# Gate and up projections of two FFNs: seven block products in place of eight

## The reference, cut to what matters

```python
D_MODEL, SEQ, D_FF = 1024, 512, 2816

def swiglu(x, w_gu, w_down):
    gu = x @ w_gu
    g, u = jnp.split(gu, 2, axis=-1)
    return (jax.nn.silu(g) * u) @ w_down

x = x + 0.5 * swiglu(rms_norm(x, g_ffn1), w_ffn1_gu, w_ffn1_down)
...
x = x + 0.5 * swiglu(rms_norm(x, g_ffn2), w_ffn2_gu, w_ffn2_down)
```

## Time and profile before

| what | us |
|---|---|
| time, median of 3 runs (1751.65 to 1751.79) | 1751.66 |
| profiled execution, its own time | 1754.53 |
| its span, first to last instruction | 1752.7 |
| PE busy in the span (9322 matmuls) | 1742.0 |
| DVE busy | 1039.4 |
| ACT busy | 760.7 |
| POOL busy | 431.9 |

### The profile page before, as it was taken

One profiled execution on the slowest core, in us unless ns is written; L12 is line 12 of the kernel. 1 busy time (PEld: TensorE's weight loads), 2 busy tenths in 40 slices (PEclk: granted clock), 3 DMA queues, 4 the chain that ended last, 5 costly groups with the idle time before them and its releaser, 6 DMA issues.

```text
span 1752.7 us, 25465 instructions
## 1 busy us (share of the span) xinstructions
PE 1742.0 (99%) x9322; PEld 1437.8 (82%) x9322; DVE 1039.4 (59%) x2178; ACT 760.7 (43%) x1413; POOL 431.9 (25%) x336
## 2 busy tenths in 40 slices
PE   9999999999999999999999999999999999999998
PEld 7778878777888888888888888889888888888887
DVE  5888867688867665555433455446756655555332
ACT  6566645556654533333232454555444322333222
POOL 4566644465553500000000332320200200000000
PEclk9999999999999999999999999999999999999999
DMA  6422123332212433333333422223321333333332
GB/s 198 138 88 73 60 61 98 95 95 79 73 49 62 138 109 96 96 96 96 106 101 106 151 64 93 85 84 103 103 64 58 96 96 96 96 96 96 109 107 85
DMA packets 54998, 166.20 MB, mean 95 GB/s; under 512 B 10264, under 2 KB 10776, under 8 KB 54904
## 3 DMA queue, kind: packets, MB, share of 16 engines
q1 hardware_dynamic: 53896, 163.69, 30.8%
q10 hardware_dynamic: 1008, 1.28, 0.2%
HBM read 162.25 MB, written 2.17 MB: 94 GB/s over the span
## 4 chain that ended last, share of the span: by engine, by line
PE 99%; DMA 0%; DVE 0%; ACT 0%; POOL 0%; SPq 0%; issue 0%; POOLq 0%
PE proj L1182 80%; PE turned L1514 2%; PE o L1536 2%; PE proj L1678 1%; PE proj L1671 1%; PE o L1779 1%; PE o L1879 1%; PE turned L1148 1%; PE turned L1758 1%; PE score L1483 1%; PE score L1868 1%; PE turned L1741 1%; PE score L1472 1%; PE score L1348 0%; PE proj L1382 0%; PE score L1741 0%
## 5 line engine op out<-in xcount | busy, mean ns | idle before, releaser
L1182 PE MATMUL proj<-hhi,whi 128*128 128x512 f32 x1456 | 580.8, 399 | 0.0
L1182 PE MATMUL proj<-hhi,wlo 128*128 128x512 f32 x1456 | 568.4, 390 | 0.0
L1182 PE MATMUL proj<-hlo,whi 128*128 128x512 f32 x1456 | 567.4, 390 | 0.0
L1970 ACT ACTIVATE whi<-ring 128x1024 fp32r<-128x1024 f32 x278 | 294.2, 1058 | 613.6 <-PE proj L1182 593.8
L2495 DVE TENSOR_TENSOR wlo<-ring,whi 128x1024 fp32r<-128x1024 f32 x199 | 243.0, 1221 | 161.7 <-ACT whi L1970 161.2
L1182 PEld LDWEIGHTS proj<-hhi,whi 128*128 128x128 f32 x1456 | 274.0, 188 | 61.3 <-issue 7.3
L1182 PEld LDWEIGHTS proj<-hhi,wlo 128*128 128x128 f32 x1456 | 273.4, 188 | 58.8
L1182 PEld LDWEIGHTS proj<-hlo,whi 128*128 128x128 f32 x1456 | 274.1, 188 | 53.0
L884 POOL TENSOR_TENSOR wlo<-ring,whi 128x512 fp32r<-128x512 f32 x160 | 213.9, 1358 | 331.7 <-ACT whi L1970 331.4
L902 POOL TENSOR_TENSOR prob<-prob 128x512 f32<-128x512 f32 x36 | 56.8, 1579 | 871.2 <-ACT prob L1966 871.2
L1996 ACT ACTIVATE prob<-prob,negmax 128x128 f32<-128x128 f32 (+3 forms) x208 | 114.0, 550 | 80.5 <-DVE negmax L2568 80.1
(11 more groups left out here) (402 smaller groups left out, 2470.1 us busy)
## 6 DMA issues: line engine op xcount, KB each, us to landing
ring<-wstream SPq DMA_DIRECT2D x285, 512.0 KB, 3.6
arena<-lines SPq DMA_DIRECT2D x28, 256.0 KB, 5.4
out<-arena SPq DMA_DIRECT2D x8, 256.0 KB, 3.3
...
```

What stands on the lines that cost most here:

```text
L1182: mm = pe.matmul(b, rounded(w), rounded(rhs(v, k)), start=(first and n == 0 and p == 0), stop=(last and n == len(blocks) - 1 and p == 2))
L1970: act.activation(rounded(dst), src, ACT.Copy, scale=scale).then_inc(ready, 1)
```

## The change

Of the 22 pairs of gate and up chunks, the first two (`PEEL`) stay as they were. For the other 20 (`SEVEN`) a pair is taken as a 2x2 block product: rows are gate and up, the contraction is split into two sets of four 128-feature blocks, and the tokens into two halves of 256. Seven products of four blocks are made in place of eight: `A11`, `S1`, `S2`, `A12`, `S3`, `S4`, `A22`, each 12 matmuls of 128x256 (four blocks, three parts). Their right sides are blocks of the activations or the combinations `T_1` to `T_4`, made once per FFN from a float32 copy `hx` of the activations (ACT `scale_h`, DVE `combine_h`, 128x1024 each; low parts of two of them on GpSimd). Their left sides are blocks of the weights or the sums `S1` to `S4`, made per pair by GpSimd (128x512 each, `seven_sums`). Each left side is rounded by ACT (`high_w`) and its low part made: `A11`, `S1`, `A12`, `A22` on VectorE (`low_w`), `S2`, `S3`, `S4` on GpSimd. PSUM sums are added up across products in place, with copies of the states in between by ACT (128x256, `copy`) and three additions by VectorE. There is one buffer for each of these operands, so the next pair's `S1` waits for PE's product `S1` of this pair (`sop_done`), and so on. A load into a pair's two ring slots now waits for the low part of `A22`. The nine early loads of `bias2` move from before the first FFN to the end of its gate and up part, and `norm_first` moves behind that part.

The diff, cut to its core (blank lines dropped):

```diff
+PEEL = 2
+SEVEN = FC - PEEL
+W_A11, W_S1, W_S2, W_A12, W_S3, W_S4, W_A22 = range(7)
+T_1, T_2, T_3, T_4 = range(4)
+HALF_S = S // 2
...
+            def load_ffn(n0, j0, f):
+                for s in range(4):
+                    sp.wait_ge(job_done, j0 + s + 1)
+                    load(stream_of(n0) + s + RING, s)
+                with sp.Fori(1, FC // 2) as i:
                     for s in range(4):
-                        sp.wait_ge(job_done, i * 4 + (j0 + s + 1))
+                        if s % 2 == 0:
+                            sp.wait_ge(slo_ready, i * 8 + (SLO + 4 * (f * SEVEN + s // 2 - 2) + 4))
                         load(i * 4 + (stream_of(n0) + s + RING), s)
+                if f == 0:
+                    sp.wait_ge(job_done, j0 + 2 * FC)
+                    sp.wait_ge(inner_done, FC)
+                    load_bias2(range(B2_EARLY))
                 load2(n0 + 2 * FC, n0 + FFN_SLOTS)
...
+            def seven_sums(i, s, n0, j0, f):
+                ahead = isinstance(i, int) and i == 0
+                g = f * SEVEN + s - 1
+                gate, up = 2 * (1 - s), 2 * (1 - s) + 1
+                pool.wait_ge(wload[up], i * 16 + 16 * (n0 // RING + 1 + s))
+                if not ahead:
+                    pool.wait_ge(sop_done, i * 12 + (SOP + 6 * (g - 1) + W_S1 + 1))
+                pool.tensor_tensor(ssum[W_S1], weight_quarter(up, 1), weight_quarter(up, 2), ALU.add).then_inc(sum_made, 1)
+                pool.wait_ge(wload[gate], i * 16 + 16 * (n0 // RING + 1 + s))
+                pool.wait_ge(sum_made, i * 8 + (SUM + 4 * g + 1))
+                if not ahead:
+                    pool.wait_ge(sop_done, i * 12 + (SOP + 6 * (g - 1) + W_S2 + 1))
+                pool.tensor_tensor(ssum[W_S2], ssum[W_S1], weight_quarter(gate, 1), ALU.add).then_inc(sum_made, 1)
+                if ahead:
+                    low_t(f, T_2)
+                else:
+                    pool.wait_ge(sop_done, i * 12 + (SOP + 6 * (g - 1) + W_S3 + 1))
+                pool.tensor_tensor(ssum[W_S3], weight_quarter(gate, 1), weight_quarter(up, 1), ALU.add).then_inc(sum_made, 1)
+                pool.wait_ge(sum_made, i * 8 + (SUM + 4 * g + 2))
+                if ahead:
+                    pool.wait_ge(job_done, j0 + 2 * PEEL)
+                else:
+                    pool.wait_ge(sop_done, i * 12 + (SOP + 6 * (g - 1) + W_S4 + 1))
+                pool.tensor_tensor(ssum[W_S4], ssum[W_S2], weight_quarter(gate, 2), ALU.add).then_inc(sum_made, 1)
+                pool.wait_ge(sum_made, i * 8 + (SUM + 4 * g + 4))
+                for w in (W_S2, W_S3, W_S4):
+                    pool.wait_ge(shi_ready, i * 14 + (SHI + 7 * g + w + 1))
+                    pool.tensor_tensor(slo[w].bitcast(F32R), ssum[w], shi[w], ALU.subtract).then_inc(pool_slo_ready, 1)
+            def low_t(f, t):
+                pool.wait_ge(thi_ready, THI + 4 * f + t + 1)
+                pool.wait_ge(t_ready, TC + 4 * f + 4)
+                pool.tensor_tensor(rounded(tlo[:, t, :]), tsum[:, t, :], thi[:, t, :], ALU.subtract).then_inc(pool_tlo_ready, 1)
+            def ffn_sums(n0, j0, f):
+                low_t(f, T_1)
+                seven_sums(0, 1, n0, j0, f)
+                with pool.Fori(1, FC // 2 - 1) as i:
+                    for s in range(2):
+                        seven_sums(i, s, n0, j0, f)
+                seven_sums(FC // 2 - 1, 0, n0, j0, f)
...
+                def seven(i, s):
+                    b = (j0 + s) % 2
+                    X, Y, Z = proj[b][:, 0:HALF_S], score[s][:, 0:HALF_S], opsum[s][:, 0:HALF_S]
+                    g = f * SEVEN + s - 2
+                    def product(to, w, parts, first):
+                        for k in range(KC // 2):
+                            for p, (weight, v) in enumerate(((shi[w], parts[0]), (shi[w], parts[1]), (slo[w], parts[0]))):
+                                mm = pe.matmul(to, rounded(weight[:, k, :]), rounded(v[:, k, :]), start=(first and k == 0 and p == 0),
+                                               stop=(k == KC // 2 - 1 and p == 2), skip_group_check=True)
+                        return mm
+                    h11, h21, h22 = ((quarter(hhi, j, l), quarter(hlo, j, l)) for j, l in ((1, 1), (2, 1), (2, 2)))
+                    t1, t2, t3, t4 = ((by_pair(thi, t), by_pair(tlo, t)) for t in range(4))
+                    pe.wait_ge(job_free[b], i * 2 + (j0 + s) // 2)
+                    pe.wait_ge(slo_ready, i * 8 + (SLO + 4 * g + 1))
+                    product(X, W_A11, h11, True).then_inc(sop_done, 1)
+                    pe.wait_ge(slo_ready, i * 8 + (SLO + 4 * g + 2))
+                    pe.wait_ge(pool_tlo_ready, PTLO + 2 * f + 1)
+                    product(Z, W_S1, t1, True).then_inc(sop_done, 1)
+                    pe.wait_ge(pool_slo_ready, i * 6 + (PSLO + 3 * g + 1))
+                    pe.wait_ge(pool_tlo_ready, PTLO + 2 * f + 2)
+                    pe.wait_ge(qc_ready, i * 8 + (QC + 4 * g + 1))
+                    product(X, W_S2, t2, False).then_inc(sop_done, 1)
+                    pe.wait_ge(slo_ready, i * 8 + (SLO + 4 * g + 3))
+                    product(Y, W_A12, h21, True).then_inc(sop_done, 1)
+                    pe.wait_ge(pool_slo_ready, i * 6 + (PSLO + 3 * g + 2))
+                    pe.wait_ge(tlo_ready, TLO + 2 * f + 1)
+                    pe.wait_ge(qc_ready, i * 8 + (QC + 4 * g + 3))
+                    product(X, W_S3, t3, False).then_inc(sop_done, 1)
+                    pe.wait_ge(pool_slo_ready, i * 6 + (PSLO + 3 * g + 3))
+                    product(Z, W_S4, h22, False).then_inc(sop_done, 1)
+                    pe.wait_ge(slo_ready, i * 8 + (SLO + 4 * g + 4))
+                    pe.wait_ge(tlo_ready, TLO + 2 * f + 2)
+                    pe.wait_ge(qc_ready, i * 8 + (QC + 4 * g + 4))
+                    product(X, W_A22, t4, False).then_inc(job_done, 2)
                 with pe.Fori(1, FC // 2) as i:
-                    up_jobs(i)
+                    for s in range(2):
+                        seven(i, s)
...
+            def scale_h(f):
+                if f == 0:
+                    act.wait_ge(gain2_ready, 1)
+                for c in range(KC):
+                    act.activation(hx[:, c, :], xT[:, c, :], ACT.Copy, scale=gain2[:, c:c + 1] if f == 0 else gain[:, G_FFN2 + c:G_FFN2 + c + 1])\
+                        .then_inc(hx_ready, 1)
...
+                def body(i, s, first=False, last=False):
+                    g = f * SEVEN + s - 2
+                    b, Z = proj[(j0 + s) % 2], opsum[s % 2]
+                    def copy(src, dst, done):
+                        act.wait_ge(sop_done, i * 12 + (SOP + 6 * g + done + 1))
+                        act.activation(dst, src[:, 0:HALF_S], ACT.Copy).then_inc(qc_ready, 1)
+                    if first:
+                        high_w(W_A22, 0, 1)
+                    else:
+                        high_w(W_A22, i, s - 1)
+                        act.wait_ge(gate_scaled, i * 2 + (GATED + g))
+                        tanh_of((s - 1) % 2, -0.5)
+                    copy(b, q1c, W_A11)
+                    if not last:
+                        high_w(W_A11, i, s)
+                    copy(Z, q5c, W_S1)
+                    if not first:
+                        high_inner(i * 2 + (s - 1), (s - 1) % 2)
+                    copy(b, v2c, W_S2)
...
+                    else:
+                        for w in (W_S1, W_S2, W_A12):
+                            high_w(w, i, s)
+                    copy(b, v3c, W_S3)
...
+                    else:
+                        for w in (W_S3, W_S4):
+                            high_w(w, i, s)
...
+                def low_w(w, i, s):
+                    g = f * SEVEN + s - 1
+                    slot = 2 * (1 - s % 2) + int(w == W_A22)
+                    if w in (W_S1, W_A22):
+                        dve.wait_ge(sum_made, i * 8 + (SUM + 4 * g + (2 if w == W_S1 else 4)))
+                    dve.wait_ge(shi_ready, i * 14 + (SHI + 7 * g + w + 1))
+                    src = ssum[w] if w in ssum else weight_quarter(slot, 2 if w in (W_A12, W_A22) else 1)
+                    dve.tensor_tensor(slo[w].bitcast(F32R), src, shi[w], ALU.subtract).then_inc(slo_ready, 1)
...
+                def gated(i, s):
+                    b, h = (j0 + s) % 2, s % 2
+                    dve.wait_ge(job_done, i * 4 + (j0 + 2 * s + 2))
+                    dve.wait_ge(tanh_ready, i * 2 + (s + DEPTH * 8 + f * FC + 1))
+                    dve.scalar_tensor_tensor(tanh[:, h, 0:HALF_S], tanh[:, h, 0:HALF_S], 1.0, proj[b][:, 0:HALF_S], ALU.subtract, ALU.mult)\
+                        .then_inc(job_free[b], 2)
+                    dve.scalar_tensor_tensor(tanh[:, h, HALF_S:S], tanh[:, h, HALF_S:S], 1.0, c22[:, :], ALU.subtract, ALU.mult)\
+                        .then_inc(ffn_step, 1)
+                    dve.wait_ge(ffn_step, i * 2 + (s + f * FC + 1))
+                    dve.tensor_tensor(tmp[:, h, :], tanh[:, h, :], tmp[:, h, :], ALU.mult).then_inc(wg_step, 1)
```

(59 more changed lines are left out.)

210 lines of the change are left out of this document (151 added, 59 removed).

## The result

The changed kernel takes 1903.04 us (median of 4 runs, 1899.66 to 1906.79) against 1751.72 for the kernel before in the same session: ratio 1.0863, interval 1.0842 to 1.0884. It is slower, as forecast, but by 151 us and not by 109, and just above the range.

What follows compares the result with a forecast made beforehand. TensorE, busy 99%, was taken to bound the kernel before; turns would bind the changed pairs. Per FFN 51.7 - 0.8 + 3.5 = 54.4, twice 109; 1751.7 + 109 = 1860 us, range 1815 to 1900 (8 in 10).

Steps and rivals of the forecast that it cites:

- The turns: Seven-product pairs: VectorE's two-SBUF and GpSimd's instructions exclude each other; 13.6 us a pair against 10.88, +51.7 us per FFN.
- the 0.4 for gaps: Seven-product pair: 0.4 us added to the 13.2 by turns for imperfect packing, giving 13.6.
- Rival D: Seven-product pairs: whole instructions are held at undisturbed lengths, 15.4 us a pair, +176 us, 1928; 3%.
- Rival C: Seven-product pairs: GpSimd alone and its waits set 10.3 to 11.5 us a pair, 1730 to 1776; 5%.
- The clock: Seven-product pairs: clock stays 1.00, TensorE's busy share 0.74 being near the 0.78 that kept it; no time added.
- rival B: Seven-product pairs: clock falls, 18 us a pair; a quarter of pairs adds 44 us, 1904, most 150, 2010; 5%.
- First and last pairs: Ends of each FFN's seven-product part: first counted among 19 pairs at 13.6 us, last at 10.05 (-0.8 us).
- The entry: First two pairs of each FFN: extra combinations and low parts may delay slot 3's low part; 3.5 us per FFN.
- TensorE's part: Seven-product pair: 84 matmuls at 0.1196 us, 10.05 us in place of 10.88; at most 33 us over 40 pairs.
- ScalarE's own work: Seven-product pair: roundings, tanh and PSUM copies take 7.2 us, which fits into TensorE's 10.05; no cost.
- bias2's loads: Nine loads ahead of the down weights in SyncE's queue: 7 us, covered by 20 us of work; nothing, at most 2.
- the clock at 1.00: Sign expected in the changed profile: granted clock at 1.00, beside GpSimd's additions at 1.6 to 1.8 us.

Runs made afterwards that it cites:

- e4_rpsum: Changed kernel with VectorE reading the norm's factor R from PSUM, not its SBUF copy, in two instructions a pair: 1817.07 us, ratio 1.0356.
- e7_tanh: Changed kernel with e4_rpsum's edit, ScalarE's v2c copy moved earlier, the entry reordered, and gating intermediates in an idle PSUM bank: 1790.69 us, ratio 1.0212.
- e8: e7_tanh with the low parts of S3 and S4 moved from GpSimd to VectorE: 1814.81 us, ratio 1.0360.
- e9: e8 with one wait more: GpSimd's next S1 sum waits for VectorE's low part of A22: 1799.37 us, ratio 1.0250.
- e10_sums: e9 with S2's low part also on VectorE, leaving GpSimd four sums, and a second wait, ahead of sum S4: 1744.33 us, ratio 0.9940.
- e3: Changed kernel with GpSimd's seven steps a pair replaced by a one-column product and memsets, sums and low parts not computed: 1734.04 us, one run.
- e2: Changed kernel with 12 unused matmuls added on TensorE ahead of product S3's waits: 1883.65 us, ratio 1.0736.

## Why the prediction was wrong in size

**The turns** were right. VectorE's two-SBUF instructions and GpSimd's hold each other, PSUM readers pass, and the undisturbed pair is 13.67 us against 13.6. So close a hit is partly luck: the 0.4 for gaps was a guess. Six versions against the sum of turns per pair (1.15 for a GpSimd instruction, 0.54 and 0.27 for VectorE's of 512 and 256 columns), with TensorE's 10.05 as the floor:

```
              GpSimd   VectorE 512+256   sum of turns   measured pair
as made       7        8 + 2             12.9           13.67 (undisturbed)
e4_rpsum      7        6 + 2             11.8           11.97
e7_tanh       7        5 + 1             11.0           11.2 to 11.4
e8, e9        5        7 + 1             9.8            12.28, 11.70
e10_sums      4        8 + 1             9.2            10.17
```

The sum is the lower end, near when GpSimd works without pause, and far off in e8 and e9, where GpSimd has pauses and starts into rows of VectorE's. The Trainium skill, page "SBUF — State Buffer", section "Who interferes with whom", has the ports that such instructions share as an exclusive lock; e3 agrees with its part on who is concerned (memsets, which read nothing there, leave VectorE at 0.69). Rival D, with whole lengths as turns, would need at least 15.4 us a pair; the undisturbed pairs of 13.67 rule it out. Rival C's 1730 to 1776 leaves out the 7 us for the entries that the other sums have.

**The clock** is the step that failed. The sum has it at 1.00, so a term for its fall is missing; I gave the fall 5%, because "the share of 0.74 is near the 0.78 that kept 1.00". The busy share of a pair was the wrong thing to compare: TensorE's idle time lies in one wait of 2.6 us in the mean and 3.48 at most, and it is behind such a wait that the clock is at 0.50 for some 3 us. The mechanism of rival B came true at a smaller price, since a fall lasts about two products and not a pair: 19 us by e2, where a quarter of the pairs at 18 us was put at 44. That the 1904 of rival B is the time measured is luck. The 36 pairs between cost 510.2 - 36 x 13.6 = 20.6 more than taken, 18 of it above the undisturbed 13.67. Without the 19 us the time is e2's 1883.65, inside the range.

**First and last pairs.** These terms were too small as well. I counted the first of each FFN among the 19 at 13.6 and the last at 10.05. They took 17.94 and 18.33, and 11.76 and 12.40: 9.1 and 4.1 us more. I had looked for the entry's price ahead of the seven products, and part of it lay in their first pair. The last has no sums for a next pair beside it, but its own three low parts: in FFN 1 GpSimd makes them from 913.66 to 918.43 us, VectorE's chain for the pair before takes turns with them, and TensorE waits 1.46 us for the copy ahead of S3.

**The entry** itself, 3.5 us per FFN taken, was about right: 9.7 lie outside the 40 pairs in all, where I had 7. TensorE's waits in the two stretches, 606 to 636 and 1455 to 1485 us (us in total, times, longest), are on the low part of slot 3, as forecast:

```profile
PE proj L1290 <- DVE wlo L2742: 2.4, 1, 2.4
PE proj L1290 <- DVE tmp L2826: 0.5, 1, 0.5
...
PE proj L1290 <- DVE wlo L2742: 3.8, 2, 2.3
```

With the turns at 101.8 as taken, 101.8 + 20.6 + 9.1 + 4.1 + 9.7 = 145.3 for the 145.1 measured. That the sum closes proves nothing by itself, since all but the first term are what was left over; the shares of turns and clock rest on e2 to e4. The median is 6 us further off than the profiled execution, which was the fastest of the four runs. Its mean granted clock was 0.970, that of the other three 0.962 to 0.965, so the clock fits here too; where it fell in them is not known.

**TensorE's part**: e3's pair of 10.08 against 10.05 worked out from a run of 12 and one of 24. ScalarE's own work, SyncE's queue, `scale_h`, bias2's loads and the ring loads I had at nothing. Outside the seven products TensorE waits in the changed kernel for nothing but the low parts above, beyond what it waited before; where it waits for ScalarE's copies inside them, ScalarE waited for VectorE. Of what I said would be seen, the clock at 1.00 did not come. GpSimd's four sums came at 1.66, 1.54, 1.37 and 1.39 us, only the first of them within the 1.6 to 1.8 named, and of VectorE's low parts those of S1 (0.74) and of most results (0.68) were hardly held; the rest came.
